# Segment exponents of a state-space scan: TensorE products replaced by decay sums that travel through DRAM

## The reference

```python
cs = jnp.cumsum((dt * a).reshape(b, nc, 128, g, r), axis=2)
seg = cs[:, :, :, None] - cs[:, :, None, :]
lmat = jnp.exp(jnp.where(lower, seg, -jnp.inf))
cb = jnp.einsum('bclgn,bcsgn->bclsg', cc, bc)
y = (jnp.einsum('bclsg,bclsgr,bcsgrp->bclgrp', cb, lmat, xc)
     + jnp.einsum('bclgn,bcgrpn,bclgr->bclgrp', cc, h_in, jnp.exp(cs)))
```

## Time and profile before

| | |
|---|---|
| median of 3 runs | 2565.73 us (2563.46 to 2565.87) |
| span of the profiled execution | 2566.1 us |
| own time of the profiled execution | no value of its own is listed; its span is 0.2 us above the highest of the three runs (2565.87 us) |
| busy: TensorE / VectorE / ScalarE / GpSimd | 2489.1 / 1224.1 / 1125.6 / 1494.5 us |
| mean granted TensorE clock | 0.993 |
| DMA | 313.03 MB, 122 GB/s mean |

### The profile page before, as it was taken

How to read it: one execution, slowest core, us unless ns; L and a number is a source line. 1 busy time by engine, 2 the same in 40 slices (tenths; PEclk the granted TensorE clock), 3 DMA queues, 4 the chain that set the end, 5 groups by cost and what they waited for, 6 DMA issues and landing times.

```text
span 2566.1 us, 39740 instructions
## 1 busy us (share of the span) xinstructions
PE 2489.1 (97%) x15548; PEld 2170.1 (85%) x15548; DVE 1224.1 (48%) x2583; ACT 1125.6 (44%) x2371; POOL 1494.5 (58%) x1318
## 2 busy tenths in 40 slices
PE   8999999999899999999999999999989999999999
PEld 7779997885688888888888888888859888889998
DVE  3545502236747888874243112121366888844210
ACT  2345533115526776774022002042364766654532
POOL 1019775870354554543975888864324666577976
PEclk9999999999999999999999999999999999999999
DMA  7566463237532222214322333332454233364564
GB/s 211 182 191 185 128 165 103 83 96 260 191 99 67 75 58 66 74 50 156 98 82 88 95 98 99 99 113 85 150 183 115 71 95 90 83 171 156 186 169 116
DMA packets 388969, 313.03 MB, mean 122 GB/s; under 512 B 12576, under 2 KB 374082, under 8 KB 387778
## 3 DMA queue, kind: packets, MB, share of 16 engines
q1 hardware_dynamic: 385874, 297.75, 39.2%
q10 hardware_dynamic: 2352, 12.59, 1.3%
q0 software_dynamic: 576, 0.43, 0.2%
HBM read 303.40 MB, written 7.34 MB: 121 GB/s over the span
## 4 chain that ended last, share of the span: by engine, by line
PE 73%; POOL 10%; DVE 7%; issue 5%; DMA 2%; ACT 2%; POOLq 1%; SPq 0%; DVEq 0%; ACTq 0%
PE PS L707 35%; PE PS L1109 10%; POOL rounded L2702 10%; PE PS L765 5%; PE PS L1116 4%; PE PS L730 2%; DVE mid_a L2445 2%; PE PS L1150 2%; PE PS L1237 2%; PE PS L658 2%; PE PS L1159 2%; PE PS L1037 1%; PE PS L929 1%; PE PS L1025 1%; PE PS L1171 1%
## 5 line engine op out<-in xcount | busy, mean ns | idle before, releaser
L2702 POOL TENSOR_TENSOR rounded<-ring,rounded 128x512 fp32r<-128x512 f32 (+1 forms) x872 | 1113.6, 1310 | 729.7 <-ACT rounded L1376 417.7
L707 PE MATMUL PS<-rounded 128*128 128x256 f32 (+1 forms) x6864 | 1135.4, 327 | 6.7 <-POOL rounded L2702 3.3
L707 PEld LDWEIGHTS PS<-rounded 128*128 128x128 f32 x6864 | 1016.6, 190 | 119.3 <-POOL rounded L2702 4.1
L2725 POOL TENSOR_TENSOR rounded<-ring,constants 128x512 fp32r<-128x512 f32 x216 | 229.3, 1092 | 248.2 <-PE PS L707 125.2
L1109 PE MATMUL PS<-rounded 128*128 128x512 f32 (+1 forms) x1536 | 343.5, 380 | 5.8 <-DVE mid_a L2445 5.1
L1109 PEld LDWEIGHTS PS<-rounded 128*128 128x128 f32 x1536 | 275.3, 188 | 61.2 <-DVE mid_a L2445 3.7
L1376 ACT ACTIVATE rounded<-ring 128x2048 fp32r<-128x2048 f32 (+1 forms) x99 | 180.0, 1822 | 136.6 <-DMA ring<-in_w_mlp_dram 55.1
L2445 DVE SCALAR_TENSOR_TENSOR mid_a<-PS,V,mid_a 128x510 f32<-128x510 f32 (+3 forms) x256 | 182.2, 714 | 25.5 <-ACT mid_a L1705 18.0
L1743 ACT ACTIVATE rounded<-constants,big 128x128 fp32r<-128x128 f32 x384 | 149.8, 390 | 0.0
L1743 ACT ACTIVATE rounded<-constants,mid_v 128x128 fp32r<-128x128 f32 x384 | 149.8, 390 | 0.0
L1116 PE MATMUL PS<-rounded 128*128 128x256 f32 x1152 | 147.8, 286 | 0.0
(11 more groups left out here) (263 smaller groups left out, 3134.2 us busy)
## 6 DMA issues: line engine op xcount, KB each, us to landing
ring<-in_w_mlp_dram SPq DMA_DIRECT2D x64, 1024.0 KB, 5.5
ring<-in_w_in_dram SPq DMA_DIRECT2D x56, 1024.0 KB, 5.4
ring<-in_ada_w_dram SPq DMA_DIRECT2D x48, 1024.0 KB, 5.2
ring<-in_w_in_dram SPq DMA_DIRECT2D x81, 512.0 KB, 4.1
ring<-in_w_up_dram SPq DMA_DIRECT2D x44, 512.0 KB, 5.1
ring<-in_w_ssd_o_dram SPq DMA_DIRECT2D x16, 1024.0 KB, 5.9
ring<-in_w_out_dram SPq DMA_DIRECT2D x12, 1024.0 KB, 5.1
ring<-in_w_down_dram SPq DMA_DIRECT2D x16, 704.0 KB, 5.0
```

What stands on the lines that cost most here:

```text
L707: mm = pe.matmul(PS[:, b, 0:cols], w[:, k, m * P:(m + 1) * P], x(half * kt + k), start=(half == 0 and k == 0 and n_pass == 0), stop=(half ...
L2702: ins = pool.tensor_tensor(lo[:, r], raw[:, r], hi[:, r], ALU.subtract)
L2725: ins = pool.tensor_tensor(hi[:, r], raw[:, r], ones[:, 0:1].broadcast_to([P, 512]), ALU.mult)
```

## The change

The sums of `dt * a` from the chunk's start (forward) or to its end (backward) are now also made as rows: `decay_sums` gets two more matmuls per chunk, whose 64 output partitions are heads and whose 128 columns are tokens. ScalarE copies them out of PSUM and stores them in DRAM. During the scan ScalarE reads, for each group and chunk, the eight rows of its heads back into all 128 partitions (`fetch`, 512 KB). It subtracts each from the head's column and clips at zero (`shift`, eight instructions of 128x128). GpSimd adds the two directions (`both_ways`, 128x512), and ScalarE makes the exponential of the negative sum and writes it into the same PSUM banks as before. TensorE's `seg` is gone, and so are the 16 copies per chunk and the rounding and splitting of `dt * a` after the fence. Two buffers of rows take turns. VectorE copies column sums over `dta` before the fence, so that `shift` has them as a per-partition operand. ScalarE takes over the waits that `seg` had: its exponential waits for `both_ways(t)`, for `cb_masked` at chunk 1, and for the weights of two chunks before; a fetch waits for the exponential that read its buffer. `states` on TensorE waits for `cb_masked` too.

```diff
+        decay_rows = [nc.dram_tensor(f"decay_rows{l}", (TT, 2 * SSD_HEADS, P), F32, kind="Internal").ap() for l in range(LAYERS)]
+        def decays_of(l, g, t):
+            of_heads = decay_rows[l][t].rearrange("(d h) n -> d (h n)", d=2)[:, g * GH * P:(g + 1) * GH * P]
+            return of_heads.unsqueeze(0).broadcast_to([P, 2, GH * P])
...
@@ TensorE: decay_sums, seg, turn_of
-                        mm = pe.matmul(PS[:, 4 + t, m:m + w], lhs, dta[:, t, r0:r0 + w], start=True, stop=True)
+                        pe.matmul(PS[:, 4 + t, m:m + w], lhs, dta[:, t, r0:r0 + w], start=True, stop=True)
+                    for d, sums in enumerate((t_le, t_ge)):
+                        r = slice(32 * d, 32 * d + 32)
+                        mm = pe.matmul(PS[r, 4 + t, 256:256 + P], dta[:, t, r], sums, start=True, stop=True)
                     mm.then_inc(*c.made(dec_ready))
...
-                def seg(t):
-                    pe.wait_ge(*c.need(seg_in, 4 * GH))
-                    if t == 1:
-                        pe.wait_ge(*c.need(cb_masked))
...
                 def states():
                     pe.wait_ge(*c.need(tok_ready, 3))
                     pe.wait_ge(*c.need(xw_ready, 6))
+                    pe.wait_ge(*c.need(cb_masked))
...
@@ ScalarE: before the fence
+                    act.activation(decay_cols[0:2 * SSD_HEADS, t, :], PS[0:2 * SSD_HEADS, 4 + t, 256:256 + P], ACT.Copy)\
+                        .then_inc(*c.made(rows_copied))
...
+                act.wait_ge(*c.sofar(rows_copied))
+                act.dma_start(decay_rows[l].rearrange("t h n -> h t n"), decay_cols[0:2 * SSD_HEADS, :, :])\
+                    .then_inc(*c.made(rows_stored, 16))
...
@@ ScalarE: in the scan
+                def fetch(g, t):
+                    act.dma_start(decay_bc[t % 2], decays_of(l, g, t)).then_inc(*c.made(decays_loaded[t % 2], 16))
+                def shift(g, t):
+                    act.wait_ge(*c.sofar(decays_loaded[t % 2]))
+                    for d in range(2):
+                        for r in range(GH):
+                            row, h = decay_bc[t % 2][:, d, r * P:(r + 1) * P], 64 + 32 * d + g * GH + r
+                            ins = act.activation(row, row, ACT.Relu, scale=-1.0, bias=by_head[:, t, h:h + 1])
+                    ins.then_inc(*c.made(seg_shifted))
+                def decays(g, t):
                     act.wait_ge(*c.need(seg_ready))
-                    act.activation(PS[:, 7 - t % 2, :], PS[:, 7 - t % 2, :], ACT.Exp).then_inc(*c.made(e_ready))
-                def segments(g, t):
...
+                    if t == 1:
+                        act.wait_ge(*c.need(cb_masked))
+                    if g or t >= 2:
+                        act.wait_ge(*c.need(m_ready))
+                    act.activation(PS[:, 7 - t % 2, :], decay_bc[t % 2][:, 1, :], ACT.Exp, scale=-1.0).then_inc(*c.made(e_ready))
+                def refetch(g, t):
+                    after = chunk_after(g, t, 2)
+                    if after:
+                        act.wait_ge(*c.sofar(e_ready))
+                        fetch(*after)
...
                     to_tok(first)
-                    decays(0)
-                    segments(g - 1, 1)
+                    decays(g - 1, 0)
+                    shift(g - 1, 1)
+                    refetch(g - 1, 0)
                     tanh_of(1 - p, 0)
                     middle(g, 1 - p, 1)
-                    decays(1)
+                    decays(g - 1, 1)
                     round_of_group(g, 3)
+                    refetch(g - 1, 1)
...
-                act.activation(dta_hi, dta, ACT.Copy).then_inc(*c.made(dta_rounded))
-                for n, t in enumerate((t_gt, t_lt)):
-                    act.activation(tri[n], t, ACT.Copy).then_inc(*c.made(dta_rounded))
+                act.wait_ge(*c.sofar(rows_stored))
+                for t in range(2):
+                    fetch(0, t)
...
@@ VectorE: before and after the fence
+                dve.wait_ge(*c.need(rows_copied, TT))
+                for d in range(2):
+                    step(dve.tensor_copy(dta[:, :, 32 * d:32 * d + 32], PS[:, 4:4 + TT, 32 + 64 * d:64 + 64 * d]))
...
-                dve.tensor_copy(dta_parts[0], dta_hi).then_inc(*c.made(dta_split))
-                dve.tensor_tensor(dta_parts[1], dta, dta_hi, ALU.subtract).then_inc(*c.made(dta_split))
...
@@ GpSimd: group
+                    def both_ways(t):
+                        pool.wait_ge(*c.need(seg_shifted))
+                        down, up = (decay_bc[t % 2][:, d, :] for d in range(2))
+                        pool.tensor_tensor(up, up, down, ALU.add).then_inc(*c.made(seg_ready))
...
+                    both_ways(0)
                     if nxt:
                         rest_of_group(2)
...
                     dtu(0)
+                    both_ways(1)
                     dtu(1)
...
                         if t + 2 < ny:
+                            both_ways(t + 2)
                             dtu(t + 2)
```

74 lines of the change are left out of this document (29 added, 45 removed).

## The result

The changed kernel takes 2592.71 us (median of four runs, 2590.25 to 2599.69) against 2565.8 before: a ratio of 1.0111, 95% interval 1.0099 to 1.0123, or 27 us more. The forecast was 2550.0 us with a range of 2523 to 2568. The profiled execution is the slowest of the four, 2599.69 us with a span of 2597.9, so 7 us of what its trace shows is more than a median run has. Its span is 31.8 us over that of before, and the trace says where: the stage of layer 0 takes 24.0 us more, that of layer 1 3.9, the stretch between them 3.0, the end 0.7, and the entry of layer 0 0.3. The stretch between the stages has no edit in it; why it grew is not shown.

The account below looks back on a forecast made before the run. Layer 0 was taken as bound by TensorE (48.5 us a turn), VectorE's loop (47.3) close behind and next to bound. Terms -7.0 - 3.0 + 1.9 - 5.6 - 3.1 + 1.0 = -15.8 us gave 2550.0 us, range 2523 to 2568.

Parts of the forecast that it names:

- -1.0 for each: Steady layer-0 turn: gains 1.0 us, from 48.5 to 47.5; seven turns give -7.0 us.
- The tightest place is the end of `taps(.., 3)`: Layer-0 turn: VectorE's taps(3) ends at 929.69, and product(0) of the next group, needing its PSUM bank, starts at 930.98.
- slack of 1.2 us: Layer 0, between taps(3) and product(0): about 1.2 us left after 0.1 us of hand-over, subtracted from VectorE's loop.
- a growth of 0.2: VectorE's layer-0 loop: -1.52 + 0.95 + 0.75 + 0.75 - 0.75 = +0.2 us against the turn before.
- The additions: GpSimd's both_ways, four a layer-0 turn: 1.04 us each, lengthening VectorE's weights they meet by 0.95 or 0.75 us.
- the wait for `states`: VectorE's layer-0 loop: its 1.52 us wait for the states products goes once the segment products are gone.
- The first turns: First turn of each layer: layer 0 at -1.0 us like other turns, layer 1 at -3.1 us.
- ScalarE's saving: ScalarE in layer 0: falls by 9 us of 36 a turn, hidden behind TensorE and VectorE.
- the 5.4 of the margin: Chunk 2's read: 5.4 us from issue until its rows are wanted, 1.3 more than a 4.1 us slab, so hidden.
- The entry of layer 0: Entry to layer 0's state-space stage: +1.9 us for extra decay_sums matmuls and short copies ahead of the fence.
- A steady turn of layer 1: Layer 1: -1.07 + 1.0 - 0.75 = -0.8 us a turn; seven turns give -5.6 us.
- the one in which every addition lands on VectorE's loop: Rival, both layers: nothing relieved, +1.4 us a layer-0 turn, +1.0 in layer 1; +17.6, 2583 us; chance 0.10.

Follow-up runs that it names:

- e3: Changed kernel with GpSimd's addition covering 8 of 512 columns, its place and waits kept: ratio 0.9972.
- e1: Changed kernel with six dummy products on TensorE between product(4) and chunk(2) in layer 0, where it waits: ratio 1.0098.
- e2: Changed kernel with both_ways(0) behind rest_of_group(2) on GpSimd in the first group of each layer: ratio 1.008.
- e10: Changed kernel, layer 0: product(5) halves around chunk(2); GpSimd's both_ways(0) behind rest_of_group(2) (layer 1: first group), rest_of_group(1) after weights(2): ratio 1.0032.
- e13: Changed kernel, GpSimd only: layer 0's rest_of_group(1) waits for weights(2), next both_ways(0) for weights(3); first groups' both_ways(0) behind rest_of_group(2): ratio 0.999.
- e5: Changed kernel with the first half of product(5) ahead of chunk(2) on TensorE in layer 0: ratio 1.0166.
- e6: Changed kernel with both_ways(0) behind rest_of_group(2) on GpSimd in every group of both layers: ratio 1.0156.
- e4: Kernel before, with seg(t) doing one of its four products and nothing else changed: ratio 0.9945.
- e8: Kernel before, with GpSimd making dtu(t) twice for t = 1, 2, 3: ratio 1.0068.

## Why the prediction was wrong

**The sum of the turn.** From the traces, per steady turn of layer 0: without the additions' work and at the full clock 47.1 us (one turn of e3), 1.4 under before; the additions take it to 50.15 (e1), +3.1; the clock to 51.4, +1.25. Six turns of +2.9 are 17.4 us, the first is +6.8, and layer 0 has its 24. The prediction had -1.0 for each.

**The step that failed first** is "The tightest place is the end of `taps(.., 3)`", with a slack of 1.2 us. That place was read rightly, but `chunk(2)` on `y_done(1)` had none and `chunk(3)` on `y_done(2)` 0.1 us, and neither was looked at. The loop that set the turn runs through them: from `masks` through VectorE to `outputs(2)`, over to TensorE at `chunk(3)`, and back to `masks`. Everything that hung on the slack went with it. VectorE's growth had nothing to fill and came out whole in the turn, 1.65 us at the full clock, where the prediction took 1.2 off a growth of 0.2.

**The additions** were sized by `dtu`, 1.04 us, and take 1.29. Their places were foretold rightly and their prices were near: `weights(0)` +1.03 (0.95), `weights(2)` +1.06 (0.75), `weights(3)` +1.1 (0.75), `weights(1)` -0.75 (-0.75), the wait for `states` gone (-1.52). Missing was the `silu` behind `weights(0)`, which has two SBUF inputs too: +0.85, which ate half of what the gone wait gave. The terms with it come to +1.8. From `masks` to the end of `taps(3)` VectorE takes 40.99 us (e1) against 39.35 before, +1.6, where the terms of the prediction came to +0.2.

**The clock** was in no step: the prediction took 1.00 from the earlier trace rows as given, though the change was about to give TensorE waits. Its price is that of the traces, up to 1.25 us a turn, and isn't clear of noise in the medians.

**The first turns** were forecast at -1.0 and -3.1 us and came out at +6.8 and +4.9. In layer 0, 4.7 of it goes when the queue goes (e2): `both_ways(0)` was placed in GpSimd's order for the steady turn, and nobody asked what it waits for in the first, where ScalarE's first shift is late. The delay itself is 1.5 us; the rest comes by the meetings that it makes (`weights(0)` 5.30 us, `weights(1)` 3.66). The remaining 2.1 is what a steady turn has with one stretch at the lower clock (50.6 in e2). In layer 1 two other traces with the same order had 39.5 us, which is +1.9, so 3 of the 4.9 may be chance.

**What held.** The wait for `states` is gone. ScalarE's saving is hidden. The shift takes 394 ns like the copy. ScalarE's exponential waits 2.98 us for `both_ways(2)` without harm to VectorE. The reads are hidden: they land in 5.1 us at the median (3.7 to 9.6), longer than the 4.1 of the earlier trace rows and at the median within the 5.4 of the margin, and no shift waited for one. The Trainium skill (DMA: Bandwidth & Descriptors, Anatomy of one DMA) led to an estimate of 3.2 us, further off than the slab's row. The page gives its fit for transfers that GpSimd issues, and these are issued by ScalarE, a condition that the prediction left out. The entry of layer 0 costs 0.3 us and not 1.9; TensorE's two extra products per chunk take 0.41. A steady turn of layer 1 gained 0.3 us, not 0.8: the terms of the prediction hold there, and what it left out is again the `silu` behind `weights(0)`, 1.25 us in place of 0.69.

**The rivals.** Nearest was the one in which every addition lands on VectorE's loop, at 2583 us and 0.10; it had the right engine and sign, and lacked the clock and the first turn. That its +1.4 us a turn is near the 1.65 of e1 is in part luck: it took off a slack of 1.2 us that wasn't there, and left out the 0.75 that `weights(1)` wins. By the page named there (the Trainium skill, SBUF — State Buffer, SBUF: two separate sides) a VectorE instruction with two SBUF inputs and a GpSimd one that reads SBUF exclude each other for their whole length. The runs fit it: the `silu` grows by 0.85 us, the four `weights(2)` by 1.06 beside an addition of 1.29, VectorE's `taps`, which read PSUM, keep their 3.1 us, and it is at times GpSimd that pays (e10's slab, 3.04 us in place of 2.56).

## What to carry to other kernels

Before work is taken off the engine that bounds a loop, list every wait of that engine in the loop and its slack, including waits that cost nothing now: the row of the releaser's end beside the row of the waiter's start. Work that is moved to GpSimd is not free on an idle GpSimd; its price is paid by VectorE's instructions with both inputs in SBUF, and it depends on the gap they fall in, so place it where VectorE reads PSUM or waits (e13: the same work, 4 us less a turn) and check the first turn and the other layer separately.

## What the runs showed of the hardware

- Of the 35 layer-0 turns in which TensorE waited 1.8 to 3.8 us in one place (after, e2, e3, e5, e6), 29 had a stretch at the lower clock and six had none. With waits of 1.01 and 0.87 us (e1), 0.66 to 0.68 twice (e4) or two of about 1.1 (e13) in a turn it stayed up (e1 from its second turn on). With a wait of 1.6 us it fell in four turns of six (e8). The lower level cost up to 1.25 us a turn on average (after against e1).
- Four `weights` that take 1.13 us alone took 3.65 beside GpSimd in steady turns and 5.30 in a first turn, and a single one up to 3.48 us.
- A read that hands the same 4 KB to 128 partitions, 512 KB in all, landed in 5.1 us at the median. In a stretch of 7 us with one such read and two weight slabs the DMA share was 0.83.
